# Expert rows fetched by indirect DMA, and the second mixing's value and receptance tiles projected later

## The reference, cut to what matters

```python
# mixture of experts: 8 experts, the two best for each token
logits = t @ w_router + b_router
top_v, top_e = lax.top_k(logits, 2);  gate = softmax(top_v)
xr = rows of t sorted by expert                     # a gather of token rows
out = (silu(xr @ w_gate[e]) * (xr @ w_up[e])) @ w_down[e]      # w: 1024 x 3584, 44 MB an expert
y = zeros.at[row_tok].add(out * row_g)              # scatter back to the tokens

# second block, first lines of its mixing (rwkv7): z = rms_norm(h) @ w_in
z = z + (prev_token(z) - z) * mu                    # token shift of r, k, v, lora columns
w, a, g = f(w0 + tanh(wl) @ w2), sigmoid(a0 + al @ a2), sigmoid(gl) @ g2
kk = normalised(k * k_k);  k = k * (1 + (a - 1) * k_a);  decay = exp(-exp(w))
S_t = S * d_t + (S @ -kk) (kk * a) + v_t k_t;  o_t = S_t @ r_t
bonus = sum(r * k * r_k, over a head's 64) * v
```

## Time and profile before

| | before |
|---|---|
| median of 3 runs | 2454.6 us |
| the profiled execution, its own time | 2454.6 us |
| its span from first to last instruction | 2452.6 us |
| PE busy | 2360.8 us (96%) |
| weight loads (PEld), beside PE | 1590.4 us (65%) |
| DVE busy | 599.1 us (24%) |
| ACT busy | 313.8 us (13%) |
| POOL busy | 143.6 us (6%) |
| read from HBM | 528.09 MB, 216 GB/s over the span |

### The profile page before, as it was taken

The page is one execution under the profiler, slowest core; times in us unless marked ns, Lnnn a source line. Parts: engine busy times, 40 slices in busy tenths (PEclk is TensorE's granted clock), DMA queues, the critical chain, the costliest instruction groups (busy, mean ns, idle before and its releaser), DMA issues. The chain is left out here.

```text
span 2452.6 us, 44903 instructions
## 1 busy us (share of the span) xinstructions
PE 2360.8 (96%) x20471; PEld 1590.4 (65%) x20471; DVE 599.1 (24%) x1351; ACT 313.8 (13%) x646; POOL 143.6 (6%) x205
## 2 busy tenths in 40 slices
PE   8999999999999989999999999999998988989998
PEld 7777788888677774535353534444456866668887
DVE  2432220002432121011010110111014265643334
ACT  0222210000231201000000000000001233110002
POOL 1000100000000103000000000000001153300000
PEclk9999999999999988999999999999999967989999
DMA  8322434336322345999999999999994110065330
GB/s 302 136 72 70 168 138 166 143 104 227 132 74 69 137 172 203 386 368 392 388 414 368 412 366 412 368 404 375 380 378 133 62 70 10 1 222 190 110 118 34
DMA packets 165402, 532.02 MB, mean 217 GB/s; under 512 B 16060, under 2 KB 31326, under 8 KB 148830
## 3 DMA queue, kind: packets, MB, share of 16 engines
q1 hardware_dynamic: 153728, 527.76, 57.1%
q10 hardware_dynamic: 11486, 1.41, 0.4%
HBM read 528.09 MB, written 1.05 MB: 216 GB/s over the span
## 5 line engine op out<-in xcount | busy, mean ns | idle before, releaser
L182 PE MATMUL bank<-hT,ring 128*128 128x256 f32 x2720 | 609.1, 382 | 4.3 <-PEq L826 2.8
L182 PE MATMUL bank<-ring,moe_he 128*32 128x512 f32 (+2 forms) x6144 | 577.0, 537 | 0.4 <-DVE moe_he L2008 0.4
L182 PEld LDWEIGHTS bank<-hT,ring 128*128 128x128 f32 x2720 | 514.5, 191 | 83.5 <-issue 13.1
L182 PEld LDWEIGHTS bank<-ring,moe_he 128*32 128x32 f32 x6144 | 199.2, 110 | 373.2 <-issue 371.4
L182 PE MATMUL bank<-ring,moe_actT 128*32 128x256 f32 x5352 | 291.7, 379 | 0.0
L182 PEld LDWEIGHTS bank<-ring,moe_actT 128*32 128x32 f32 x5352 | 173.8, 110 | 116.7 <-issue 3.4
L2062 DVE TENSOR_TENSOR moe_act<-moe_silu,bank 128x512 f32<-128x512 f32 (+2 forms) x48 | 26.8, 614 | 537.5 <-PE bank L182 537.5
L182 PE MATMUL bank<-ring 128*128 128x256 f32 x384 | 86.0, 386 | 6.8 <-DVE ring L631 6.8
L182 PEld LDWEIGHTS bank<-ring 128*128 128x128 f32 x384 | 73.9, 193 | 17.7 <-issue 7.3
L182 PE MATMUL bank<-cffn_act,ring 128*128 128x256 f32 x352 | 79.7, 379 | 0.4 <-DVE cffn_act L1495 0.4
L182 PE MATMUL bank<-ffn_act,ring 128*128 128x256 f32 x352 | 79.4, 379 | 0.0
(11 more groups left out here) (690 smaller groups left out, 2039.8 us busy)
## 6 DMA issues: line engine op xcount, KB each, us to landing
ring<-in_moe_w_down SPq DMA_DIRECT2D x55, 2048.0 KB, 14.3
ring<-in_moe_w_gate SPq DMA_DIRECT2D x32, 2048.0 KB, 16.3
ring<-in_moe_w_up SPq DMA_DIRECT2D x32, 2048.0 KB, 11.0
ring<-in_w_in SPq DMA_DIRECT2D x29, 2048.0 KB, 8.5
ring<-in_moe_w_gate SPq DMA_DIRECT2D x28, 1536.0 KB, 8.9
ring<-in_moe_w_up SPq DMA_DIRECT2D x28, 1536.0 KB, 8.7
ring<-in_w_up SPq DMA_DIRECT2D x10, 2048.0 KB, 9.8
ring<-in_w_out SPq DMA_DIRECT2D x6, 2048.0 KB, 7.9
```

What stands on the lines that cost most here:

```text
L182: ins = pe.matmul(out, lhsT, rhs, start=start, stop=stop, **kw)
```

## The change

1. **Experts.** `h_tok` is stored in the order (token, column group, column) and written once to a DRAM tensor `h_rows` of 1024 rows of 1 KB, by an SP DMA at the start of the block, ahead of the slabs. For experts 1 to 7, `gather` is replaced: `locate(e + 1)`, two products of `token` (4 times the token's number, alike in all 128 columns) with `sel` of 96 columns, now ahead of `scatter(e - 1)`; `located` on DVE, three small operations that keep each partition's own slot and add the column group; and on POOL three indirect DMAs of 128 rows of 1 KB each into `picked`, one for each group. DVE's `gathered` waits for these and transposes from SBUF. Expert 0 keeps `gather`. POOL builds `token` and `part` after its masks.
2. **Second mixing, project.** The r tiles are made one by one in the tail: the first after the compressed scores, the second after the gates, the third after the transposes. The v tiles leave this block, and so do the three bonus (`dot`) products. lora is made between the compressed branch's hidden layer and the norms. The slabs' order and slots follow.
3. **Second mixing, attend.** Rounds 1 to 3 end with a v tile each (ACT copies it, DVE shifts it: `late_copy`, `late_shift`), rounds 4 and 5 with an s5 tile each, round 4 with the three bonus products too. v is transposed after round 6. `sw = v * bonus` is DVE's last work of the block.

```diff
 # plan_second
-    m.use_slots([0, 1, 2, 3])
-    for key, c, n in (("kv", C2_KC, 512), ("r", 0, 384), ("k", 384, 384), ("v", 768, 384), ("lora", C2_WL, 256),
-                      ("q", C2_Q, 384), ("kw", C2_KW, 274), ("s5", C2_S5, 256)):
+    m.use_slots([0, 1, 2, 3, 2, 0, 1, 3, 0, 1])
+    for key, c, n in (("kv", C2_KC, 512), ("k", 384, 384), ("lora", C2_WL, 256), ("q", C2_Q, 384), ("kw", C2_KW, 274),
+                      ("r", 0, 384), ("v", 768, 384), ("s5", C2_S5, 256)):
 # experts, PE
+            def locate(e):
+                pe.wait_ge(token_ready.sem, 1)
+                pe.wait_ge(sel_ready.sem, e)
+                for t in range(TT):
+                    m.mm(pe, m.bank[4][:, 0:CAP], x.token[:, t, :], x.sel[:, t, :], t == 0, t == TT - 1,
+                         gath if t == TT - 1 else None)
...
+                if e + 1 < N_EXPERTS:
+                    locate(e + 1)
                 if e:
                     scatter(e - 1)
-                if e + 1 < N_EXPERTS:
-                    gather(e + 1)
 # experts, DVE
+            def located(e):
+                v.wait_ge(gath.sem, e + 1)
+                diag = x.diag[:].rearrange("p (g n) -> p g n", g=1).broadcast_to([P, GRP, 32])
+                k.step(v.tensor_tensor(x.found[:], m.bank[4][:, 0:CAP].rearrange("p (g n) -> p g n", g=GRP), diag, ALU.mult))
+                k.step(v.tensor_reduce(x.where[:], x.found[:], AX.X, ALU.add))
+                v.tensor_scalar(x.index[:, e % 2, :], x.where[:].rearrange("p g a -> p (g a)"), x.part[:], None, ALU.add)\
+                    .then_inc(index_ready.sem, 1)
...
+                if e + 1 < N_EXPERTS:
+                    located(e + 1)
                 if e:
                     add(e - 1)
 # experts, POOL, after the masks
+            g.wait_ge(m.load_in[2], 16 * 7)
+            for e in range(1, N_EXPERTS):
+                g.wait_ge(index_ready.sem, e)
+                g.wait_ge(he_ready.sem, e)
+                for j in range(GRP):
+                    g.indirect_dma_start(x.picked[:, j, :], None, x.rows_of_h,
+                                         bass.IndirectOffsetOnAxis(ap=x.index[:, e % 2, j:j + 1], axis=0)).then_inc(picked.sem, 16)
 # experts, SP
+            sp.dma_start(x.rows_of_h.rearrange("(t p c) n -> p t (c n)", t=TT, c=4), x.h_tok).then_inc(m.load_in[2], 16)
             m.issue(sp, m.number[("2", "kv")])
 # project
-    ORDER = (("kv", 5), ("r", 3), ("swap", 3), ("k", 3), ("v", 3), ("norm", 3), ("lora", 2), ("q", 3), ("kw", 4), ("up", 9),
-             ("swap_w", 1), ("gates", 9), ("turned", 3))
+    ORDER = (("kv", 5), ("swap", 3), ("k", 3), ("lora", 2), ("norm", 3), ("q", 3), ("kw", 4), ("up", 9), ("r0", 1),
+             ("swap_w", 1), ("gates", 9), ("r1", 1), ("turned", 3), ("r2", 1))
...
 # project, ACT: the second r tile's copy stands ahead of the exponential of the compressed scores
                     for j in range(9):
                         copy(gb[:, j, :])
+                    raw_in(6)
                     act.wait_ge(s_in.sem, 1)
                     act.activation(S[:, :, 0:N_CMP], S[:, :, 0:N_CMP], ACT.Exp).then_inc(x_ready.sem, 1)
 # project, DVE, last lines
+                    shift(2, "r2", 0)
+                    s.step(v.tensor_tensor(bonus, bonus, r, ALU.mult))
+                    s.step(v.tensor_tensor(r, r, grown, ALU.mult))
                     v.wait_ge(o_ready.sem, 1)
 # attend, PE
+                    def late_round(n):
+                        if n <= 4:
+                            pe.wait_ge(x_out.sem, 2 * n)
+                        if n <= 3:
+                            project("v", n - 1, m.bank[6][:, 0:T], late_ready)
+                            if n == 3:
+                                m.done_with_slab()
+                        elif n <= 5:
+                            if n == 5:
+                                pe.wait_ge(late_out.sem, 4)
+                            else:
+                                for p in range(3):
+                                    o = m.bank[7][:, p * T:(p + 1) * T] if p < 2 else m.bank[6][:, T:2 * T]
+                                    pe.matmul(o, m.pair_ones[:], bonus[:, p, :], start=True, stop=True, skip_group_check=True)
+                            project("s5", n - 4, m.bank[6][:, 0:T], late_ready)
...
-                        if n in (1, 3):
-                            pe.wait_ge(x_out.sem, 2 * n)
-                            state_input(n // 2)
+                        late_round(n)
+                    pe.wait_ge(mat_out.sem, 8)
+                    pe.wait_ge(late_in.sem, 3)
+                    for t in range(TT):
+                        for p in range(3):
+                            ins = pe.transpose(m.bank[6 + t][:, p * P:(p + 1) * P], vch[:, p, t * P:(t + 1) * P], m.ident[:])
+                        turned.on(ins)
 # attend, DVE
+                    def late_shift(u):
+                        v.wait_ge(late_out.sem, u + 1)
+                        k.step(v.tensor_tensor(vch[:, u, :], late[:, u % 2, 0:T], late[:, u % 2, 1:T + 1], ALU.subtract))
+                        k.step(v.scalar_tensor_tensor(out=vch[:, u, :], in0=vch[:, u, :], scalar=par(m, "shift_mu_2", 0, 6 + u),
+                                                      in1=late[:, u % 2, 1:T + 1], op0=ALU.mult, op1=ALU.add), late_in)
...
+                        if n <= 3:
+                            late_shift(n - 1)
+                    v.wait_ge(late_out.sem, 5)
+                    v.tensor_tensor(self.sw, vch, bonus, ALU.mult)
```

More of the change, by code:

```diff
@@ L1544, in __init__ @@
         self.iota = sb("iota", [P, CAP])
+        self.picked = spare[:, 2 * D:2 * D + GRP * T].rearrange("p (g n) -> p g n", g=GRP)
+        self.token = spare[:, 2 * D + GRP * T:3 * D].rearrange("p (t n) -> p t n", t=TT)
+        self.diag, self.part = sb("diag", [P, 32]), sb("part", [P, 1])
+        self.found, self.where = sb("found", [P, GRP, 32]), sb("where", [P, GRP, 1])
+        self.index = sb("index", [P, 2, GRP], mybir.dt.uint32)
+        self.rows_of_h = m.nc.dram_tensor("h_rows", [4 * T, T], F32, kind="Internal").ap()
         self.slot = sb("slot", [P, GRP])
@@ L1581, in __init__ @@
         self.upi, self.low = spare[:, SLAB - 2 * P:SLAB - P], spare[:, SLAB - P:SLAB]
[L1582 removed]
+        self.fib = [spare[:, 3 * D + 512 + 256 * i:3 * D + 512 + 256 * (i + 1)].rearrange("p (a n) -> p a n", a=NT) for i in range(2)]
         self.Bn = [spare[:, 3 * D + 256 * i:3 * D + 256 * (i + 1)].rearrange("p (a b n) -> p a b n", a=NT, b=2) for i in range(2)]
@@ L2267, in _ @@
                     m.done_with_slab()
-                    for j in range(3):
-                        feature("r", j * P)
-                    m.done_with_slab()
                     pe.wait_ge(consts.sem, 1)
@@ L2303, in _ @@
                         single(m.pair_ones[:], t1[:, p, :])
-                    for j in range(2):
-                        feature("lora", j * P)
-                    m.done_with_slab()
                     for j in range(3):
@@ L2333, in _ @@
                         single(gsel[:, j, :], gl)
-                    pe.wait_ge(dot_in.sem, 1)
-                    for p in range(3):
-                        ins = pe.matmul(half(6 + p // 2, p % 2), m.pair_ones[:], t2[:, p, :], start=True, stop=True)
-                    ins.then_inc(dot_ready.sem, 1)
+                    feature("r", P)
                     pe.wait_ge(p_ready.sem, 1)
@@ L2481, in _ @@
                     for j in range(3):
-                        shift(j, "r", j)
-                    for j in range(3):
                         shift(3 + j, "k", j)
@@ L2487, in _ @@
                     s.step(ins, kk0)
-                    for j in range(3):
-                        shift(6 + j, "v", j)
+                    for j in range(2):
+                        shift(9 + j, "lora", j)
                     moved(v, "norm", 3)
@@ L2493, in _ @@
                     s.step(v.tensor_tensor(kk, kk, t1, ALU.mult))
-                    for j in range(2):
-                        shift(9 + j, "lora", j)
                     moved(v, "up", 9)
@@ L2527, in _ @@
                     s.step(ins, p_ready)
+                    shift(1, "r1", 0)
                     s.step(v.tensor_reduce(self.nfh, self.levels, AX.X, ALU.max, negate=True))
-                    v.wait_ge(dot_ready.sem, 1)
-                    for p in range(3):
-                        ins = v.tensor_tensor(sw[:, p, :], vch[:, p, :], half(6 + p // 2, p % 2), ALU.mult)
-                    s.step(ins)
                     v.wait_ge(exps.sem, 3)
-                    s.step(v.tensor_tensor(r, r, t2, ALU.mult))
                     s.step(v.tensor_tensor(t3, t3, kk, ALU.mult))
```

124 lines of the change are left out of this document (77 added, 47 removed).

## The result

| | before | changed |
|---|---|---|
| median | 2454.6 us (4 runs, 2447.3 to 2463.2) | 2474.0 us (4 runs, 2473.2 to 2477.6) |
| the profiled execution: span, clock | 2452.6 us, 0.970 | 2475.9 us, 0.962 |

The ratio is 1.0071 (95% interval 1.0043 to 1.0099): 19.5 us slower, where 14.3 us faster was forecast. Both belong to the result.

What follows compares the result with a forecast made beforehand. The experts were taken to be bound by PE, with DMA close behind. Experts -14.8, project -9.5 and attend +10 summed to -14.3 us from 2454.6, giving 2440.3 us, with the range 2431 to 2457.

Steps and rivals of the forecast that it cites:

- Attend: Second mixing's attend block: v tiles, bonus products and waits, less a steadier clock; +10 us taken, +8.5 with the clock held.
- a round with such a wait took 10.14 in place of 9.49, and two more rounds get it: +1.3: Attend's rounds: late_shift ahead of divide on DVE waits for the v tile, costing +1.3 us over two more rounds.
- the mixing costs: Second mixing: clock falls in both project's tail and an attend round; project -3, attend +14, total 2451 us; chance 0.15.
- The reason for staying nearer the high clock: Attend: +10 us was taken nearer +8.5 than +13.8 because after an s5 tile the clock held for 12 us.
- Project: Second mixing's project block: -20.7 us from the dense part, +11.2 in the tail, so -9.5 us; bounds -14 and -3.
- Experts: Seven experts: locate at 0.5 us of PE replaces the gather's 2.61 us, saving 14.8 us; bounds 11.3 and 15.5.
- Neither rival: Experts: indirect DMAs' rows come late, 2482 us, chance 0.12; or DMA becomes the bound, 2455 us, chance 0.05.

Runs made afterwards that it cites:

- changed_timed: The changed kernel, unedited, timed again beside the kernel before; its profile is the third of the changed kernel: 2453.7 us against 2455.0, ratio 0.9999.
- shift_again: Repeat of the changed kernel with late_shift moved behind the two divides of the next round on DVE: 2435.9 us (one run).
- mixing_only: The kernel before with only the second mixing's part of the change (slots' order, project, attend): 2465.9 us, ratio 1.0056.
- experts_only: The kernel before with only the experts' part of the change (locate, indirect DMAs, rows_of_h): 2453.1 us, ratio 0.9986.

## Why the prediction was wrong

**Attend is the step that failed**, in its term "a round with such a wait took 10.14 in place of 9.49, and two more rounds get it: +1.3". I read the earlier trace rows for the price of DVE standing behind a v or s5 tile. They show something else. Round 2 has an s5 tile ahead of it (2004.62 to 2009.81) and took 9.49 us, because DVE did divide beside the tile; round 3 has none, so its divide lay open, and PE waited 0.87 us:
```profile
2006.17 0.29 DVE L2762 TENSOR_SCALAR ring<-ring,sec_sum 128x128 f32<-128x128 f32 x1
2006.37 0.73 DVE L2763 TENSOR_SCALAR ring<-ring,sec_sum 128x256 f32<-128x256 f32 x1
...
2021.75 0.55 PE L2658 MATMUL bank<-ident,ring 128*128 128x128 f32 x3 [0.87 <-DVE ring L2763]
```
The 10.14 us are the price of a round without a tile. late_shift, on DVE ahead of divide, could only start when the tile and its copy were done, so divide slid from behind the tile to in front of the turn. I named the wait and did not ask what had hidden divide, nor what POOL would be doing then. The waits are 5.5 us in sum, 4 times my figure; the rest is the clock, which fell after each of the three in two executions, and after the first two in the third. Measured: late_shift's place costs 22.5 us of attend in the first profile and 17.8 in the third (114.9 and 110.2 against 92.4). Without it the other terms came out in sum: +7.2 us (92.4 against 85.2), and the forecast with the clock held, +8.5, is 7.2 without its 1.3. That it fits so closely is luck: the first v tile took 6.1 us in place of 3.65, round 3 gained 0.65 that I had not counted, and before's attend has taken 80.3 to 93.2 us.

The rival "the mixing costs" was right on attend with a size too small: +14, where +25 to +30 came. It supposed one round at the half clock, not three and their tiles. Its other half, -3 for project, did not come. The reason for staying nearer the high clock, that after an s5 tile it held for 12 us, was read from rounds in which PE never waited for divide behind a tile.

**Project**: forecast -9.5, measured -8.2 in the first profile and -12.2 to -12.4 in nearly all others. The working stands; from the first r tile on the granted clock was 0.92 in changed_timed, which came near the lower bound of -14, and 0.77 in the first profile.

**Experts**: the gather's 2.61 us for locate's 0.61 is 2.0 us per expert (forecast 2.1), and the whole stage gives 13.7 us where the hole is absent (forecast 14.8). Neither rival came: rows landed 5.9 to 7.9 us after each issue, PE never waited for `moe_he` after the first expert, and it never waited for a slab while 394 GB/s were drawn. What I had no term for is the hole and what goes with it, 0.5 to 1.4 us per expert, that took 6 to 9 us back in three groups of runs of six. Why indirect transfers disturb PE and DVE at some times and not at others stays open. The kernel alone does not decide it, nor the chip alone; issuing later moved the hole and did not end it, and it came without a late `add` too. The number of transfers and their kind could not be told apart.

Sum for the first pair of profiles: +6.4 ahead of the experts (unchanged code; the clock dips at other places), -4.5, -8.2, +29.7 make +23.3 us, the difference of the spans. For changed_timed: +4.1, -13.7, -12.4, +25.0, -2.7 make +0.3, the spans being 0.5 apart, and its ratio of 0.9999 agrees. Where all my terms but attend's are met, then, the change is worth nothing; with attend's order mended, some 20 us (shift_again, one run: 2435.9 against 2458.2).

## What to carry to other kernels

Before you put work on an in-order queue behind a late result, list what stands behind it there and where that work is hidden now; if it is hidden behind the very tile you wait for, put the new work after it. In rounds like these, of short products with small waits, a wait can cost several times its length (5.5 us of waits cost 17.8 to 22.5 here), so count idle stretches and not only busy time, and look for a dense tile to put into the longest of them. When a new kind of transfer is used, time the same file in more than one group of runs: here one file was worth 0.1% in one and 0.8% in another.

## What the runs showed of the hardware

- TensorE's clock fell in every round of attend with a wait of 1.78, 2.36, 2.42 or 5.92 us between short products, and held through a round with one of 1.30. After 0.79 us it went either way: in round 4 of the changed kernel it fell in two executions (attend 114.9) and held in the third and in mixing_only (110.2). So it did after 0.87 us in round 3 of the unchanged code: it held in the kernel before and fell in experts_only. In the changed kernel a fall cost a round some 4 us beside the wait, and the v tile behind it 1.3 to 1.9.
- DVE operations stretch beside POOL's: a scaling of 128x128 from 0.29 to 1.85 us, five of 128x200 from 1.46 to 4.60 us in all. The two longest took 1.32 and 1.85 us there and ended 0.1 us behind POOL's.
- An indirect DMA of 128 pieces of 1 KB keeps POOL 0.95 us, with 0.30 between two; three plain ones took 1.59 us in all. Indirect ones land 5.9 to 7.9 us after issue, with 394 GB/s drawn in all.
- In some groups of runs three indirect DMAs went with a start of DVE's next operation 1.8 to 2.6 us behind the scatter's end (0.07 otherwise) and with 0.5 to 1.2 us more of PE's time in the seam, in others with neither, with the same code.
